# Memory attention of the second block: values as the weights of TensorE, one product per pair of heads

## The chip, the core and the metric

The program runs on one core of one Trainium2 chip. The metric is the device time of one execution in microseconds (us); the median of three runs of the kernel before is 1542.08 us (1541.72 to 1542.87).

## What is computed

Two transformer blocks, one after the other, on 512 tokens of width 1024, all in float32. The change lies in the second block, in the attention of the tokens to a memory of 256 vectors (4 heads of width 64):

```
qm = rmsnorm_2(qm, q_gain).astype(f32)
km = rmsnorm_2(km, k_gain).astype(f32)
logits = jnp.einsum('bqhd,bmhd->bhqm', qm, km) * (MEM_DH_2 ** -0.5)
p = jax.nn.softmax(logits, axis=-1)
out = jnp.einsum('bhqm,bmhd->bqhd', p, vm.astype(f32))
```

Its output (256 columns of the 1024 of `mixed`) is joined with two other mixers' outputs and multiplied by `w_out`: `x = x + mixed @ w_out`.

## The kernel before

Each engine runs its own instruction stream; semaphores order them. TensorE (PE) does nearly all of its work as products of a float32 matrix split in a high and a low part: one tile product is three instructions (L1952 to L1954, in the helper `product`) of 256 or 512 moving columns in the replicated float32 format. Products of plain float32 operands (scores, transposes, values) are issued as two instructions each, transposes as one.

The stretch of the change is the loop `attention("mem_2", ...)` of block 2, written once per engine. It runs in steps s = 0 to 35. There are 32 **units** of (head, tile of 128 queries). Units 0 to 15 are the memory attention ("mem_2"; pairs of heads f = 0, 1, so units 0 to 7 are pair 0), units 16 to 31 the causal attention ("sa"; 1 to 4 tiles of keys each). At step s, in this order:

- PE makes the scores of unit s (L2114; for "mem_2" both heads of a pair at the even steps, L2121 for "sa"), transposes the probabilities of unit s - 3 (L2129) into bank 6, the only transpose bank, makes the value product of unit s - 4 (L2141) in bank 7, the output bank, and then four tile products (12 instructions) of the projections `hi` and `hg` (steps 0 to 31). From step 17 on, `tail` adds pieces of the recurrent mixer at the end of a step, all in bank 1.
- VectorE (DVE) takes the maximum of the scores (L1392, L1394; L1404, L1408 for "sa"), at odd steps divides the outputs of two units by their sums (L1416, L1418) and writes them into `mix`, and then does one round of the top-key search of the sparse mask (L1722, L1723; steps 1 to 22). At steps 4 and 6 it also multiplies `qf` (L1818).
- ScalarE (ACT) copies the transposed probabilities of unit s - 3 from bank 6 to `pT` (L733), takes the exponentials of unit s with their sum (L749), and then does the step's work for the projections: copies, the rounding of a load of weights (L644 at steps 8, 16, 24) and its negation for a DMA that adds (L651).

A value product in the kernel before takes the transposed probabilities of one unit (128 keys x 128 queries, twice) as weights and 64 columns of values as moving operand:

```
for c in range(keys // P):
    v_ = vv(unit, h, c)
    ins = nc.tensor.matmul(B(("O", u_))[:, values(u_, v_.shape[-1])], tb[u_ % 2][:, c, :], v_,
                           start=c == 0, stop=c == keys // P - 1)
```

so its output has tokens on the partitions, and `mix` has to be turned to features for `w_out`. `mix_turn(j)` (L2537, four transposes each) does that for the eight column tiles j: the two of the memory attention, j = 0 and 1, at the ends of steps 32 and 33, the other six after the loop, once DVE has written the last tiles of the recurrent mixer (L1858, semaphore `hg_scaled`).

The attention of block 1 has the other form already: `att_outputs` (L2286, L2293) spreads the inverse sums of a pair of heads over a bank by four transposes, and then uses 64 columns of values as weights and the probabilities as moving operand, the two heads of the pair in the two halves of the output partitions, with c from 0 to 3 and 512, 384, 256 and 128 moving columns.

`plan_banks` numbers the uses of the eight PSUM banks; `claim(key)` waits until the bank's earlier uses are free, `ready(key)` until PE is done with it, `frees(key, ins)` frees it.

## Time and profile before

| | |
|---|---|
| median of 3 runs | 1542.08 us (1541.72 to 1542.87) |
| the profiled execution, its own time | 1541.8 us |
| its span (first to last instruction) | 1540.0 us |
| PE busy | 1521.7 us, 99% |
| DVE busy | 860.6 us, 56% |
| ACT busy | 641.3 us, 42% |
| the loop of the change, PE | about 1030.3 to 1129.7 us |

A row of the timeline gives the start from the beginning of the span, the time until the row's last instruction ends, the engine, the line, the operation and how many instructions were merged. An instruction of PE shows the time until its result is there, and the next one starts long before that; what an instruction costs PE is therefore read from one start to the next, not from its duration. An idle time of over 0.15 us ahead of a row stands in brackets, with what ended it.

### The profile page before, as it was taken

To read this page: it belongs to the slowest core of one execution; us is meant where nothing else is said; L and a number is where in the kernel's file an instruction comes from. 1 tells how busy PE (TensorE), PEld (TensorE's weight loads), DVE (VectorE), ACT (ScalarE), POOL (GpSimd) and SP (SyncE) were. 2 spreads that over 40 slices of the span, in tenths; PEclk is the share of its full clock that TensorE was granted. 3 is DMA by queue.
4 is the path that set the end of the run, shared out by engine and by line. 5 is a ranking of instruction groups with operands and counts; after the bars stand their busy time and mean duration, and the time that the engine had idled before them with its cause. 6 is when DMAs were issued, how large, how long until landed. Compare 5 with 4: busy or idle time off the path is not lost. (4 is left out here: it accounts for less than half of the span.)

```text
span 1540.0 us, 20083 instructions
## 1 busy us (share of the span) xinstructions
PE 1521.7 (99%) x7670; PEld 1268.5 (82%) x7670; DVE 860.6 (56%) x1321; ACT 641.3 (42%) x888; POOL 24.1 (2%) x32
## 2 busy tenths in 40 slices
PE   7999999999999999999999999999999999999999
PEld 7888667888888888888888868999888888888887
DVE  5443565444456877777434778878564543444222
ACT  6442444322245444444333555686653322322210
POOL 0000000000000000000000000010000000000000
PEclk9999999999999999999999999999999999999999
DMA  9313212232233133222333223254312322222232
GB/s 363 132 55 109 103 56 82 83 109 94 98 113 133 55 110 109 83 107 82 137 109 128 69 83 113 56 124 106 91 65 82 110 84 107 87 103 96 95 109 82
DMA packets 25386, 158.33 MB, mean 103 GB/s; under 512 B 2819, under 2 KB 3331, under 8 KB 8300
## 3 DMA queue, kind: packets, MB, share of 16 engines
q1 hardware_dynamic: 23228, 150.01, 27.5%
q0 software_dynamic: 2016, 7.34, 2.5%
q8 instruction: 42, 0.69, 0.2%
q14 instruction: 20, 0.16, 0.0%
q10 hardware_dynamic: 80, 0.13, 0.0%
HBM read 147.87 MB, written 2.13 MB: 97 GB/s over the span
## 5 line engine op out<-in xcount | busy, mean ns | idle before, releaser
L1202 DVE TENSOR_TENSOR w_lo<-raw,w_hi 128x2048 fp32r<-128x2048 f32 x109 | 249.8, 2292 | 347.3 <-ACT w_hi L644 347.2
L1952 PE MATMUL bank<-h_hi,w_hi 128*128 128x512 f32 x1096 | 431.5, 394 | 1.1 <-DVE cy L1544 0.8
L1954 PE MATMUL bank<-h_hi,w_lo 128*128 128x512 f32 x1096 | 427.0, 390 | 0.0
L1953 PE MATMUL bank<-h_lo,w_hi 128*128 128x512 f32 x1096 | 426.7, 389 | 0.0
L644 ACT ACTIVATE w_hi<-raw 128x2048 fp32r<-128x2048 f32 x123 | 235.0, 1910 | 321.7 <-PE bank L1954 307.4
L1952 PEld LDWEIGHTS bank<-h_hi,w_hi 128*128 128x128 f32 x1096 | 205.6, 188 | 45.3 <-issue 2.8
L1954 PEld LDWEIGHTS bank<-h_hi,w_lo 128*128 128x128 f32 x1096 | 205.3, 187 | 43.7
L1953 PEld LDWEIGHTS bank<-h_lo,w_hi 128*128 128x128 f32 x1096 | 205.5, 188 | 42.0 <-issue 0.2
L1952 PE MATMUL bank<-a_hi,w_hi 128*128 128x512 f32 x352 | 136.9, 389 | 0.0
L1953 PE MATMUL bank<-a_lo,w_hi 128*128 128x512 f32 x352 | 136.9, 389 | 0.0
L1954 PE MATMUL bank<-a_hi,w_lo 128*128 128x512 f32 x352 | 136.9, 389 | 0.0
L1952 PE MATMUL bank<-w_hi,h_hi 128*128 128x256 f32 x320 | 97.0, 303 | 0.5 <-ACT tok L682 0.3
L1954 PE MATMUL bank<-w_hi,h_lo 128*128 128x256 f32 x320 | 90.3, 282 | 0.0
L1953 PE MATMUL bank<-w_lo,h_hi 128*128 128x256 f32 x320 | 90.2, 282 | 0.0
L1953 PEld LDWEIGHTS bank<-a_lo,w_hi 128*128 128x128 f32 x352 | 66.1, 188 | 13.8
L1954 PEld LDWEIGHTS bank<-a_hi,w_lo 128*128 128x128 f32 x352 | 66.1, 188 | 13.7
L1952 PEld LDWEIGHTS bank<-a_hi,w_hi 128*128 128x128 f32 x352 | 66.1, 188 | 13.7
L1952 PE MATMUL bank<-br_hi,w_hi 128*128 128x512 f32 (+1 forms) x160 | 62.5, 390 | 0.5 <-DVE br_lo L1272 0.5
L1952 PEld LDWEIGHTS bank<-w_hi,h_hi 128*128 128x128 f32 x320 | 60.9, 190 | 1.9 <-issue 0.7
L1953 PE MATMUL bank<-br_lo,w_hi 128*128 128x512 f32 (+1 forms) x160 | 62.3, 389 | 0.0
L1954 PE MATMUL bank<-br_hi,w_lo 128*128 128x512 f32 (+1 forms) x160 | 62.2, 389 | 0.0
L1953 PEld LDWEIGHTS bank<-w_lo,h_hi 128*128 128x128 f32 x320 | 61.1, 191 | 0.9 <-issue 0.7
(315 smaller groups left out, 2005.2 us busy)
## 6 DMA issues: line engine op xcount, KB each, us to landing
raw<-weights SPq DMA_DIRECT2D x128, 1024.0 KB, 4.8
w_lo<-raw POOLq DMA_DIRECT2D x14, 512.0 KB, 5.0
toep<-bias_scratch SPq DMA_DIRECT2D x8, 448.0 KB, 4.6
x<-xT SPq DMA_DIRECT2D x2, 1024.0 KB, 12.7
x_tok<-x_tok SPq DMA_DIRECT2D x1, 2048.0 KB, 13.8
mem2T<-mem2T SPq DMA_DIRECT2D x2, 1024.0 KB, 5.3
outT<-x SPq DMA_DIRECT2D x8, 256.0 KB, 4.2
lead<-lead SPq DMA_DIRECT2D x2, 512.0 KB, 4.7
```

The costliest lines, as they stand in the source:

```text
L644: nc.scalar.activation(w_hi[PLACE[m]][:, :], raw[m % 2][:, :], ACT.Copy).then_inc(hi_ready, 1)
L1202: nc.vector.tensor_tensor(w_lo[PLACE[m]][:, :], raw[m % 2][:, :], w_hi[PLACE[m]][:, :].bitcast(F32), ALU.subtract).then_inc(lo_ready, 1)
L1952: nc.tensor.matmul(o, lh, rh, start=first, stop=False)
L1953: nc.tensor.matmul(o, lh, rl, start=False, stop=False)
L1954: return nc.tensor.matmul(o, ll, rh, start=False, stop=last)
```

## The change

The 16 value products of the memory attention are taken out of steps 4 to 19. In their place, once per pair of heads f:

- DVE inverts the sums of the pair's eight units and spreads them over 512 columns (`inverse_2`) at steps 9 and 17;
- PE turns that into bank 7 by four transposes ("R2") at the start of steps 10 and 18, and ACT copies the bank into `mix` after the exponentials of the same step;
- PE makes the pair's output ("O2") in the same bank at the start of steps 11 and 19: values as weights (64 columns), probabilities of four query tiles as 512 moving columns, head e in partitions 64e to 64e + 63;
- DVE multiplies the output by the spread inverse sums at steps 12 and 20, in place, in `mix`, which now holds features on the partitions for these two tiles.

The divisions by the sums for these units (L1416, L1418 at the odd steps 5 to 19) are gone, and so are `mix_turn(0)` and `mix_turn(1)`; the rounding of these two tiles reads `mix` instead of a bank. The first value product of "sa" (unit 16, step 20) now waits until bank 7 is freed by DVE's second multiplication.

```diff
@@ -194,8 +194,12 @@
             use(("T", w), T_BANK)
-            if kind == "mem_2":
+            if kind == "mem_2" and s >= SAH * TT:
                 use(("O", w), O_BANK)
+            elif kind == "mem_2":
+                if s % (2 * TT) == 2 * TT - 1:
+                    use(("R2", s // (2 * TT)), O_BANK)
+                    use(("O2", s // (2 * TT)), O_BANK)
             elif s % GROUP[kind] == GROUP[kind] - 1:
@@ -252,7 +256,8 @@
     tiles("o_hg", TT, (TAIL_BANK,))
-    tiles("turn_mix", KT)
+    for j in range(2, KT):
+        use(("turn_mix", j), j % 4)
     tiles("w_out_2", KT, (4, 5, 0, 1), first=FIRST["w_out_2"], per=2)
@@ -395,6 +400,8 @@
         row_2 = [at(f"row_2{s}", AR + (72 + 2 * s) * K, [S]) for s in range(NLP)]
+        pT_pair = [at(f"pT_pair{e}", AR + (20 + 24 * e) * K, [MT, S]) for e in range(2)]
+        inverse_2 = at("inverse_2", AR + 96 * K, [S])
         pT_2 = [at(f"pT_2{s}", AR + (46 + 50 * s) * K, [TT, P]) for s in range(2)]
@@ -432,7 +439,7 @@
         p_ready = sem("p_ready")
-        inverse_ready = sem("inverse_ready")
+        inverse_ready, inverse_2_ready = sem("inverse_ready"), sem("inverse_2_ready")
         bias_saved = sem("bias_saved")
@@ -727,11 +734,19 @@
                         ready(("T", w))
-                        if w >= UNIT0[kind] + 2:
-
-                            ready(("O", w - 2))
+                        unit, h, i, _ = UNITS[w]
+                        if unit == "mem_2":
+                            if w >= UNIT0["mem_2"] + 2 * TT:
+                                ready(("O2", 0))
+                            copy_to = pT_pair[h % 2][:, :, i * P:(i + 1) * P]
+                        else:
+                            if w >= UNIT0["sa"] + 2:
+                                ready(("O", w - 2))
+                            else:
+                                ready(("O2", 1))
+                            copy_to = tb[w % 2][:, 0:keys // P, :]
                         frees(("T", w), nc.scalar.activation(
-                            tb[w % 2][:, 0:keys // P, :], B(("T", w))[:, 0:keys].rearrange("p (c t) -> p c t", t=P),
+                            copy_to, B(("T", w))[:, 0:keys].rearrange("p (c t) -> p c t", t=P),
                             ACT.Copy))
@@ -746,8 +761,18 @@
                         scale = q_root[:, int(unit == "mem_2"), 0, SAH * i + h:SAH * i + h + 1]
+                        total = mx[:, w % 8, 2:3]
+                        if unit == "mem_2":
+                            f = s // (2 * TT)
+                            total = sums[:, f, s % (2 * TT):s % (2 * TT) + 1]
                         nc.scalar.activation(rb[w % NLP][:, 0:keys], src, ACT.Exp, bias=mx[:, w % 8, 1:2], scale=scale,
-                                             accum_out=mx[:, w % 8, 2:3]).then_inc(exp_ready, 1)
+                                             accum_out=total).then_inc(exp_ready, 1)
+                    if s in (2 * TT + 2, 4 * TT + 2):
+                        f = (s - 2) // (2 * TT) - 1
+                        ready(("R2", f))
+                        frees(("R2", f), nc.scalar.activation(
+                            mix[:, :, MIX_MEM + f * P:MIX_MEM + (f + 1) * P],
+                            B(("R2", f))[:, :].rearrange("p (t d) -> p t d", d=P), ACT.Copy))
                     if between is not None:
@@ -1138,7 +1163,12 @@
                 if s > 2 * SAH * TT:
-                    turned("turn_mix", (s - 2 * SAH * TT - 1,), lambda j: mo_hi[:, j, :])
+                    j = s - 2 * SAH * TT - 1
+                    if j < 2:
+                        wait_own(("O2", j))
+                        nc.scalar.activation(mo_hi[:, j, :].rearrange("p (t d) -> p t d", d=P),
+                                             mix[:, :, MIX_MEM + j * P:MIX_MEM + (j + 1) * P], ACT.Copy
+                                             ).then_inc(rounded, 1)
@@ -1407,7 +1437,21 @@
                                                 ).then_inc(neg_max, 1)
-                    if s >= LAG + 1:
+                    if s in (2 * TT + 1, 4 * TT + 1):
+                        f = (s - 1) // (2 * TT) - 1
+                        dve.wait_ge(exp_ready, UNIT0["mem_2"] + 2 * TT * (f + 1))
+                        link(nc.vector.reciprocal(sums[:, f, :], sums[:, f, :]))
+                        nc.vector.tensor_copy(inverse_2[:, :].rearrange("p (u d) -> p u d", d=64),
+                                              sums[:, f, :].unsqueeze(2).to_broadcast([P, 2 * TT, 64])
+                                              ).then_inc(inverse_2_ready, 1)
+                    if s in (2 * TT + LAG + 1, 4 * TT + LAG + 1):
+                        f = s // (2 * TT) - 1
+                        wait_free(("R2", f))
+                        ready(("O2", f))
+                        pair_ = mix[:, :, MIX_MEM + f * P:MIX_MEM + (f + 1) * P]
+                        frees(("O2", f), nc.vector.tensor_tensor(
+                            pair_, B(("O2", f))[:, :].rearrange("p (t d) -> p t d", d=P), pair_, ALU.mult))
+                    if s >= SAH * TT + LAG + 1:
                         w = UNIT0[kind] + s - LAG - 1
@@ -1860,7 +1904,10 @@
                 if s > 2 * SAH * TT + 1:
-                    turned("turn_mix", (s - 2 * SAH * TT - 2,), lambda j: mo_hi[:, j, :], lambda j: mo_lo[:, j, :])
+                    j = s - 2 * SAH * TT - 2
+                    low_part(mo_lo[:, j, :].rearrange("p (t d) -> p t d", d=P),
+                             mix[:, :, MIX_MEM + j * P:MIX_MEM + (j + 1) * P],
+                             mo_hi[:, j, :].rearrange("p (t d) -> p t d", d=P))
@@ -2101,6 +2148,26 @@
                 for s in range(count + LAG + 1):
+                    if s in (2 * TT + 2, 4 * TT + 2):
+                        f = (s - 2) // (2 * TT) - 1
+                        claim(("R2", f))
+                        pe.wait_ge(inverse_2_ready, f + 1)
+                        for i in range(TT):
+                            ins = nc.tensor.transpose(B(("R2", f))[:, i * P:(i + 1) * P],
+                                                      inverse_2[:, i * P:(i + 1) * P], ident[:, :])
+                        done(("R2", f), ins)
+                    if s in (2 * TT + LAG, 4 * TT + LAG):
+                        f = (s - LAG) // (2 * TT) - 1
+                        last = ("T", UNIT0["mem_2"] + 2 * TT * (f + 1) - 1)
+                        claim(("O2", f))
+                        pe.wait_ge(bank_free[slot[last].bank], turn(last) + 1)
+                        for c in range(MT):
+                            for e in range(2):
+                                h = 2 * f + e
+                                ins = nc.tensor.matmul(B(("O2", f))[64 * e:64 * e + 64, :],
+                                                       vm[:, c, h * DH:(h + 1) * DH], pT_pair[e][:, c, :],
+                                                       start=c == 0, stop=c == MT - 1)
+                        done(("O2", f), ins)
                     if LAG <= s < count + LAG and UNITS[UNIT0[kind] + s - LAG][0] == "mem_2":
@@ -2129,7 +2196,7 @@
                         done(("T", u_), ins)
-                    if s >= LAG + 1:
+                    if s >= SAH * TT + LAG + 1:
                         u_ = UNIT0[kind] + s - LAG - 1
@@ -2551,9 +2618,6 @@
                 tail(s - TAIL)
-                if s in (2 * SAH * TT, 2 * SAH * TT + 1):
-                    pe.wait_ge(bank_free[O_BANK], turn(("O", UNIT0["sa"] - 1)) + 1)
-                    mix_turn(s - 2 * SAH * TT)
             wait_all("turn_mq", range(2))
             pe.wait_ge(padded, 4)
```

The line numbers of the changed kernel are higher (L2129 is L2196, L2141 is L2208). Three places in the order of instructions:

**PE, steps 9 to 11.** Before, step 10 begins with the scores (L2114), and each step has transposes (L2129) and a value product (L2141):
```order
L2129 MATMUL bank<-ident,row_m_173 128x128 [waits exp_ready,bank_free6]
L2129 MATMUL bank<-ident,row_m_173 128x128
L2141 MATMUL bank<-vm,pT_180 128x64 [waits bank_free6]
L2141 MATMUL bank<-vm,pT_180 128x64
...
L2114 MATMUL bank<-kmT_even,mqT 128x256 [waits exp_ready,bank_free0]
L2114 MATMUL bank<-kmT_odd,mqT 128x256
L2129 MATMUL bank<-ident,row_m_174 128x128 [waits exp_ready,bank_free6]
L2129 MATMUL bank<-ident,row_m_174 128x128
L2141 MATMUL bank<-vm,pT_179 128x64 [waits bank_free6,bank_free7]
L2141 MATMUL bank<-vm,pT_179 128x64
...
L2129 MATMUL bank<-ident,row_m_171 128x128 [waits exp_ready,bank_free6]
L2129 MATMUL bank<-ident,row_m_171 128x128
```
In the changed kernel (L2196 transposes, L2181 scores):
```order
L2196 MATMUL bank<-ident,row_m_173 128x128 [waits exp_ready,bank_free6]
L2196 MATMUL bank<-ident,row_m_173 128x128
...
L2156 MATMUL bank<-ident,inverse_181 128x128 [waits inverse_2_ready,bank_free7]
L2156 MATMUL bank<-ident,inverse_181 128x128 x3
L2181 MATMUL bank<-kmT_even,mqT 128x256 [waits exp_ready,bank_free0]
L2181 MATMUL bank<-kmT_odd,mqT 128x256
L2196 MATMUL bank<-ident,row_m_174 128x128 [waits exp_ready,bank_free6]
L2196 MATMUL bank<-ident,row_m_174 128x128
...
L2167 MATMUL bank<-pT_pair_179,vm 64x512 [waits bank_free6,bank_free7]
L2167 MATMUL bank<-pT_pair_180,vm 64x512
L2167 MATMUL bank<-pT_pair_179,vm 64x512
L2167 MATMUL bank<-pT_pair_180,vm 64x512
```
The value products are gone; four transposes of `inverse_2` stand ahead of the scores of step 10, and a product of 64 weight columns and 512 moving columns, four times, ahead of the transposes of step 11.

**ACT and DVE, step 10 and what leads to it.** ACT in the changed kernel, from the transposed copy of step 9 to that of step 11:
```order
L748 ACTIVATE pT_pair_179<-bank 128x2x128 [waits bank_ready6]
L768 ACTIVATE row_m_172,sums<-bank,mx,q_root 128x256 [waits bank_ready6,neg_max]
L658 ACTIVATE w_lo_57<-w_hi_55 128x1024 [waits hi_ready]
L748 ACTIVATE pT_pair_180<-bank 128x2x128 [waits bank_ready6]
L768 ACTIVATE row_m_173,sums<-bank,mx,q_root 128x256 [waits bank_ready6,neg_max]
L773 ACTIVATE mix<-bank 128x4x128 [waits bank_ready7]
L689 ACTIVATE v_hg<-bank,st 128x256 [waits bank_ready2]
L658 ACTIVATE w_lo_57<-w_hi_55 128x1024
L748 ACTIVATE pT_pair_179<-bank 128x2x128 [waits bank_ready7,bank_ready6]
```
The copy of "R2" (L773) stands behind the exponentials of step 10 (L768). DVE in the changed kernel, steps 8 to 10:
```order
L1422 TENSOR_REDUCE mx<-bank 128x2 [waits bank_ready5,dve_step]
L1424 TENSOR_TENSOR mx<-mx,q_root 128x2 [waits dve_step]
L1766 MAX st<-sel 128x8
L1767 MATCH_REPLACE sel<-st,sel 128x512 [waits dve_step]
L1443 RECIPROCAL sums<-sums 128x8 [waits exp_ready,dve_step]
L1444 COPY inverse_181<-sums 128x512 [waits dve_step]
L1766 MAX st<-sel 128x8
L1767 MATCH_REPLACE sel<-st,sel 128x512 [waits dve_step]
L1422 TENSOR_REDUCE mx<-bank 128x2 [waits bank_ready0,dve_step]
L1424 TENSOR_TENSOR mx<-mx,q_root 128x2 [waits dve_step]
```
The reciprocal and the spread of the sums (L1443, L1444) stand at step 9, behind the search round of step 8, where L1416 and L1418 stood before.

**DVE and PE, step 20.** DVE in the changed kernel:
```order
L1434 ISA row_175,mx<-bank,sel 128x256 [waits bank_ready6,bank_ready4,dve_step]
L1434 ISA mx 128x1
L1438 TENSOR_SCALAR mx<-mx,q_root 128x1 [waits bank_free4]
L1452 TENSOR_TENSOR mix<-bank,mix 128x4x128 [waits bank_ready7,bank_free7]
L1766 MAX st<-sel 128x8
```
PE in the changed kernel (L2577 is a piece of `tail`, the end of step 19):
```order
L2577 MATMUL bank<-ident,kk 128x128 [waits bank_free1]
L2577 MATMUL bank<-ident,kk 128x128 x3
L2188 MATMUL bank<-skT_even,sqT 128x256 [waits bank_free4]
L2196 MATMUL bank<-ident,row_176 128x128 [waits exp_ready,bank_free6]
L2208 MATMUL bank<-sv,pT_182 128x64 [waits bank_free6,bank_free7]
```
DVE's multiplication (L1452) stands behind the mask and maximum of the scores of step 20 (L1434, L1438), and PE's first value product (L2208) waits for bank 7.

## Rows read from the trace of the kernel before

**Rows 1.** The page, parts 1 and 2: busy time, granted clock
```profile
PE 1521.7 (99%) x7670; PEld 1268.5 (82%) x7670; DVE 860.6 (56%) x1321; ACT 641.3 (42%) x888; POOL 24.1 (2%) x32
...
PEclk9999999999999999999999999999999999999999
```

**Rows 2.** Timeline of PE, step 5 (start us, us, engine, line, op, xcount)
```profile
1040.89 0.28 PE L1954 MATMUL bank<-w_hi,h_lo 128*128 128x256 f32 x1
...
1041.23 0.56 PE L2141 MATMUL bank<-vm,pT 128*128 128x64 f32 x4
...
1041.80 0.28 PE L1953 MATMUL bank<-w_lo,h_hi 128*128 128x256 f32 x1
```

**Rows 3.** Timeline of PE, step 3, which has no value product
```profile
1036.28 0.28 PE L1954 MATMUL bank<-w_hi,h_lo 128*128 128x256 f32 x1
...
1036.73 0.28 PE L1953 MATMUL bank<-w_lo,h_hi 128*128 128x256 f32 x1
```

**Rows 4.** Line L2141 alone: count, ns min/median/max, first and last start
```profile
L2141 PE MATMUL bank<-vm,pT x64: 222/275/275, 1039.1 to 1077.2; 128*128 128x64 f32 x64
```

**Rows 5.** Timeline of PE in block 1, the products of one pair of heads
```profile
196.13 0.65 PE L2293 MATMUL bank<-pT_att,v 128*64 128x512 f32 x2
...
195.60 0.60 PE L2286 MATMUL bank<-ident,inverse 128*128 128x128 f32 x4
196.13 2.38 PE L2293 MATMUL bank<-pT_att,v 128*64 128x512 f32 x16
198.44 0.50 PE L1952 MATMUL bank<-h_hi,w_hi 128*128 128x512 f32 x1
```

**Rows 6.** Timeline of DVE, steps 5 to 9
```profile
1042.77 0.17 DVE L1416 RECIPROCAL mx<-mx 128x2 f32<-128x2 f32 x1
...
1043.24 0.55 DVE L1722 MAX8 st<-sel 128x8 f32<-128x384 f32 x1
...
1050.23 0.69 DVE L1392 TENSOR_REDUCE mx<-bank 128x2 f32<-128x512 f32 x1
...
1052.61 0.17 DVE L1416 RECIPROCAL mx<-mx 128x2 f32<-128x2 f32 x1
```

**Rows 7.** Timeline of PE, DVE and ACT, steps 10 and 12
```profile
1053.25 0.60 PE L2114 MATMUL bank<-kmT_even,mqT 128*128 128x256 f32 x2
...
1054.37 0.44 PE L2129 MATMUL bank<-ident,row_m 128*128 128x128 f32 x2
...
1058.62 0.60 PE L2114 MATMUL bank<-kmT_even,mqT 128*128 128x256 f32 x2
...
1059.48 0.38 PE L2129 MATMUL bank<-ident,row_m 128*128 128x128 f32 x2
...
1059.75 0.69 DVE L1392 TENSOR_REDUCE mx<-bank 128x2 f32<-128x512 f32 x1 [0.64 <-PE bank L2114]
...
1060.74 0.57 ACT L749 ACTIVATE row_m<-bank,mx,q_root 128x256 f32<-128x256 f32 x1 [0.46 <-DVE mx L1394]
```

**Rows 8.** Lines L1370, L851 and L1341 alone, block 1
```profile
L1370 DVE COPY inverse<-sums x4: 426/428/429, 167.1 to 239.3; 128x512 f32<-128x512 f32 x4
...
L851 ACT ACTIVATE spread_inv<-bank x4: 576/577/597, 181.5 to 242.1; 128x512 f32<-128x512 f32 x4
...
L1341 DVE TENSOR_TENSOR q<-bank,spread_inv x4: 680/692/692, 182.1 to 248.0; 128x512 f32<-128x512 f32 x4
```

**Rows 9.** Timeline, step 20
```profile
1079.22 0.60 PE L2121 MATMUL bank<-skT_even,sqT 128*128 128x256 f32 x2
...
1079.95 0.42 DVE L1404 CUSTOM_DVE_ANT_0 row<-bank,sel 128x256 f32<-128x256 f32 x1 [0.56 <-DVE sel L1723]
...
1080.55 0.69 DVE L1722 MAX8 st<-sel 128x8 f32<-128x512 f32 x1
```

**Rows 10.** Timeline, end of the loop
```profile
1127.42 2.18 DVE L1858 SCALAR_TENSOR_TENSOR mix<-mix,st,g_tok 128x128 f32<-128x128 f32 x8
...
1129.65 0.31 PEld L2537 LDWEIGHTS bank<-ident,mix 128*128 128x128 f32 x3 [0.23 <-DVE mix L1858]
```

## The prediction

> **What bounds the kernel now.** I read the page first: PE is busy in 99% of the span at full granted clock, DVE and ACT in 56% and 42% [rows 1]. So every instruction that leaves PE's stream shortens the run by its cost there, and every new wait of PE lengthens it, unless the stretch ends on another engine. Then I read the timeline of the loop that changes. PE's starts follow each other without a hole through nearly all of it; DVE, too, has no hole from 1042.77 to past 1052.61 us [rows 6]. At the loop's end PE waits 0.23 us for DVE's last L1858 [rows 10]. Those two facts decide this case: in the middle a second engine is full, and the end belongs to DVE.
>
> **The sum, part by part**, against the profiled execution's 1541.8 us, which lies 0.3 us under the median.
>
> *Value products taken out.* From the last projection instruction ahead of the transposes to the second one behind them PE takes 0.91 us with a value product (1040.89 to 1041.80) [rows 2] and 0.45 us without (1036.28 to 1036.73) [rows 3]. A unit's value product, four instructions of 64 columns, costs 0.46 us. There are 64 such instructions [rows 4], 16 units: -7.3 us.
>
> *Pair products put in.* The changed kernel has not been seen, but block 1 makes the same product, 64 weight columns, the two heads in two halves of the partitions. The first two of its instructions, 512 columns each, are both done 0.65 us after the first began [rows 5]; one after another two instructions of only 256 columns take 0.60 us [rows 7]. So the two halves run side by side. The 16 instructions are eight side-by-side couples of 512, 512, 384, 384, 256, 256, 128 and 128 columns, 2560 in all, from 196.13 to 198.44: 0.90 ns a column. A pair in the new place has four couples of 512: 2048 x 0.90 = 1.85 us, and 0.09 us ahead of the first (the transposes end at 195.60 + 4 x 0.11 = 196.04). Two pairs: +3.8 us. If the halves ran one after another it would be 4096 columns at 0.84 ns (the scores' 256 columns in half of 0.43 us, from the 0.86 us of the four at 1058.62 to 1059.48 [rows 7]), 3.4 us a pair. I take the first, since it is the same form.
>
> *Sums spread.* Four transposes per pair, 0.11 us each: +0.9 us for two pairs. `mix_turn` 0 and 1, eight transposes of the same size, leave PE: -0.9 us, but at steps 32 and 33. The first transposes behind the loop start at 1129.65 because DVE's eight L1858 run from 1127.42 to 1129.60 without a hole [rows 10], and nothing in DVE's chain waits for `mix_turn`. PE just arrives 0.9 us earlier and waits 0.9 us longer: I cost the removal at 0 (between -0.9, if DVE's chain shortened too, and 0).
>
> *First wait, step 10.* PE gets there six value products earlier: 1053.25 - 6 x 0.46 = 1050.5. It now wants `inverse_2`. DVE has lost L1416 with L1418 of steps 5 and 7, 0.47 us each (1042.77 to 1043.24), so its step 9 begins at 1052.61 - 0.93 = 1051.68; the search rounds and the two `qf` products ahead of it are not shorter, and the scores of step 8 reach DVE in time (it began them at 1050.23, two us behind PE). Reciprocal 0.25 and the spread copy 0.43 us [rows 8]: 1052.4. PE stands still from 1050.5 to 1052.4: +1.9 us. The wait that PE had in this step, 1053.25 + 0.86 to 1054.37, is gone with it: -0.26 us.
>
> *Second wait, step 11.* The pair product needs bank 7, which ACT frees behind the exponentials of step 10. From PE's first scores to DVE's maximum 1.13 us, from there to the exponentials 0.99 us [rows 7], 0.57 us for them, 0.58 us for the copy [rows 8]: 3.3 us after the scores started. PE needs 0.86 us for scores, 0.22 for transposes and 1.43 for twelve projection instructions: 2.5 us. +0.8 us. Of the ACT work queued behind (copy of `v_hg`, negation) nothing is late for PE by more than that.
>
> *The same two at steps 18 and 19.* DVE has lost two more odd-step divisions by then and has no `qf` product: PE's step 12 starts 1.1 us later than before (eight value products of 0.46 less; 0.44 + 1.9 - 0.26 + 0.8 + 1.9 more), at 1059.7. DVE's maximum follows at 1060.9 [rows 7], and up to `inverse_2` of step 17 DVE has, in a row: two maxima of two units (0.87 each), the multiplication of the first pair (0.69 [rows 8]), five search rounds (1.51 each, 1052.61 - 0.87 - 1050.23 [rows 6]), two masked maxima (0.60 at most [rows 9]) and the spread of the sums (0.68): 1072.5 to 1072.8. PE, which loses six more value products on the way, is there at about 1072.2: a wait of 0.3 to 0.6 us, of which I take 0.3 because these masked maxima have half the columns. ACT's copy behind the exponentials of step 18 is 0.8 us late again, as at step 11: together +1.1 us.
>
> *Fifth wait, step 20.* PE's first value product of "sa" needs bank 7 free. Before, DVE reached L1404 0.73 us after the scores' start and the next instruction at 1.33 us [rows 9]. The multiplication stands there now, 0.69 us [rows 8], so the bank is free 2.05 us after the scores' start; PE is ready after 0.54 us: +1.5 us. After that DVE and PE meet again at the end of the same step (DVE waits for the state product), so nothing of it is carried on, up or down.
>
> The sum: -7.3 + 3.8 + 0.9 + 0 + 1.9 - 0.3 + 0.8 + 1.1 + 1.5 = +2.4 us; the tenths are uncertain, and of the places I did not cost (a copy of `kT` behind a later ACT, PE's entry into the half-width product from projections) all can only add, so I say +2.6 us, **1544.7 us** from the median of 1542.1.
>
> A page speaks against the change more strongly. By the Trainium skill, "TensorE: Matmul & The Clock Gate", section "Back-to-back issue gap", a stream of matmuls is spaced by the moving columns, about 60 cycles for up to 64 columns and 518 for 512. By that table alone the 64 instructions would give back an estimated 1.6 us and the sum would come to about +8 us. The same section adds that the load of weights shares in the spacing, and this case's trace shows that side: an instruction of 64 columns is 0.11 us, as much as a transpose of 128.
>
> **The rivals.**
> 1. *The waits don't come.* DVE or ACT are earlier than I think, or the semaphores cost less: then -7.3 + 3.8 + 0.9 - 0.3 = -2.9 us, with the tail's 0.9 us -3.8 us: 1538.3 to 1539.2. For it: DVE is only 56% busy, and three of the waits are guarded by a step's distance. Against: DVE is full in just this stretch, and the copy and the multiplication stand behind work that starts from the same step's scores. Faster by over 0.2%: 0.12, and with some of the waits only, about no change: part of "same".
> 2. *The halves run one after another* in this place: 2 x (3.4 - 1.9) = +3.0 us on top, 1547.7. Against it rows 5. Chance 0.05.
> 3. *The columns decide.* If the old instructions were worth only their columns, 64 x 64 x 0.84 ns = 3.4 us instead of 7.3, the sum would be +6.3: 1548.4. Rows 2 and 3 measure just this difference, so 0.02. This is the case in which the page's table above would hold.
> 4. *The waits come larger*: one in the middle of a saturated DVE pushes the exponentials, and PE waits for its next transposes as well; a lower granted clock after a hole of 1.9 us would do the same (before, the clock stays full throughout [rows 1]). One more wait of 0.8 us puts it beyond the bound: 1545.5 to 1547. Chance 0.28.
> 5. *The change does less than it says*: the turns are gone from the stream but not from the time. That is in my forecast already.
>
> **How the numbers follow.** A measurement of this kernel can tell about 0.2%, 3.1 us, from no change: from 1539.0 to 1545.2. The forecast (all five waits as computed, give or take 0.5 us) has a chance of 0.53, and it lies within the bound, 0.5 us from its upper end. Faster 0.12 from rival 1; slower 0.35 from rivals 2, 3 and 4. The range leaves out the far half of rival 1 and most of rivals 2 and 3: 1540.6 to 1547.6.
>
> **What would show it.** L2141 of "mem_2" gone, steps 4 to 9 of PE 0.46 us shorter each; PE idle before L2156 at step 10, ended by DVE's copy, about 1.9 us; idle before L2167 twice, ended by ACT's copy L773, about 0.8 us; idle before L2208 at step 20, ended by DVE L1452, about 1.5 us; L2167 eight instructions per pair in 1.9 us, couples at the same start; the first transposes behind the loop started by DVE as before, with PE waiting over 1 us. Wrong it is if PE starts L2156 at step 10 without a hole (rival 1), or if eight L2167 take over 3 us (rival 2).

## The result and the profile after

The changed kernel takes **1544.89 us** (median of 14 runs, 1543.72 to 1546.72), the kernel before in the same series 1541.74 us (1541.1 to 1542.87): ratio 1.0021, 95% interval 1.0014 to 1.0028. It is 3.1 us slower, and the interval, 2.2 to 4.3 us, leaves no change out, though the difference is only 0.2% of the time. Predicted were 1544.7 us.

The page of the changed kernel, parts 1 and 2, against [rows 1]:

```profile
span 1543.1 us, 19956 instructions
...
PE 1519.4 (98%) x7622; PEld 1262.5 (82%) x7622; DVE 859.5 (56%) x1311; ACT 641.9 (42%) x890; POOL 24.1 (2%) x32
...
PEclk9999999999999999999999999999999999999999
```

PE has 2.3 us less to do and the span is 3.1 us longer: PE stands still more. The clock is full in every slice, as before. Where it stands still the view of PE's waits says, for 1049 to 1084 us (line <- what it waited for: us in total, times, longest). For the kernel before it lists nothing in the same time.

```profile
PE bank L2156 <- DVE inverse L1444: 1.8, 1, 1.8
PE bank L2208 <- DVE mix L1452: 1.4, 1, 1.4
PE bank L2167 <- ACT mix L773: 1.2, 2, 0.7
```

In the changed kernel the spread transposes are L2156, the pair products L2167, the value products of "sa" L2208, the turns L2604, the three lines of a tile product L1999 to L2001, DVE's spread copy L1444, its multiplication L1452, ACT's copy of the spread sums L773.

The bracket of a row counts from the modelled end of the instruction before. I take a **hole** as start to start less the usual distance: 0.12 us behind a product instruction (see 1050.47 and 1050.59 below), 0.11 behind a transpose. The timeline at the first two places, and what ended each wait:

```profile
1050.47 0.28 PE L1999 MATMUL bank<-w_hi,h_hi 128*128 128x256 f32 x1
1050.59 0.28 PE L2000 MATMUL bank<-w_lo,h_hi 128*128 128x256 f32 x1
1050.71 0.28 PE L2001 MATMUL bank<-w_hi,h_lo 128*128 128x256 f32 x1
...
1051.24 0.68 DVE L1767 MATCH_REPLACE8 sel<-st,sel 128x512 f32<-128x512 f32 x1
...
1051.95 0.20 DVE L1443 RECIPROCAL sums<-sums 128x8 f32<-128x8 f32 x1
1052.19 0.43 DVE L1444 COPY inverse<-sums 128x512 f32<-128x512 f32 x1
...
1052.77 0.30 PE L2156 MATMUL bank<-ident,inverse 128*128 128x128 f32 x1 [1.77 <-DVE inverse L1444]
...
1055.36 0.56 ACT L768 ACTIVATE row_m<-bank,mx,q_root 128x256 f32<-128x256 f32 x1
1055.62 0.28 PE L2001 MATMUL bank<-w_hi,h_lo 128*128 128x256 f32 x1
...
1055.91 0.58 ACT L773 ACTIVATE mix<-bank 128x512 f32<-128x512 f32 x1
...
1056.55 1.94 PE L2167 MATMUL bank<-pT_pair,vm 128*64 128x512 f32 x8 [0.66 <-ACT mix L773]
...
1058.42 0.33 PE L2196 MATMUL bank<-ident,row_m 128*128 128x128 f32 x1
```

Step 10: PE is ready at 1050.71 + 0.12, DVE comes out of its search round at 1051.9, and the transposes start at 1052.77: a hole of 1.94 us. Step 11: 1056.55 - 1055.62 - 0.12 = 0.81 us. The pair product itself takes 1058.42 - 1056.55 = 1.87 us. The same at steps 18 and 19, and step 20:

```profile
1072.22 0.60 PE L2577 MATMUL bank<-ident,kk 128*128 128x128 f32 x4
...
1072.94 0.52 PE L2156 MATMUL bank<-ident,inverse 128*128 128x128 f32 x3
...
1075.27 0.65 PE L2577 MATMUL bank<-ident,kk 128*128 128x128 f32 x4
...
1076.49 1.94 PE L2167 MATMUL bank<-pT_pair,vm 128*64 128x512 f32 x8 [0.57 <-ACT mix L773]
...
1081.10 0.27 PE L2196 MATMUL bank<-ident,row 128*128 128x128 f32 x1
...
1082.00 0.68 DVE L1452 TENSOR_TENSOR mix<-bank,mix 128x512 f32<-128x512 f32 x1
...
1082.73 0.32 PE L2208 MATMUL bank<-sv,pT 128*128 128x64 f32 x1 [1.36 <-DVE mix L1452]
```

Four transposes of L2577 take 0.44 us, so the holes are 1072.94 - 1072.66 = 0.28 us and 1076.49 - 1075.71 = 0.78 us; step 20 has 1082.73 - 1081.21 = 1.52 us. And the end of the loop, which answers to [rows 10]:

```profile
1128.65 0.42 DVE L1894 SCALAR_TENSOR_TENSOR g_tok<-th,g_tok 128x256 f32<-128x256 f32 x1 [0.93 <-ACT th L1151]
1128.99 1.13 DVE L1902 SCALAR_TENSOR_TENSOR mix<-mix,st,g_tok 128x128 f32<-128x128 f32 x4
...
1130.29 0.29 DVE L1462 TENSOR_TENSOR mix<-bank,mx 128x128 f32<-128x128 f32 x1
...
1130.50 2.18 DVE L1902 SCALAR_TENSOR_TENSOR mix<-mix,st,g_tok 128x128 f32<-128x128 f32 x8
1130.64 2.00 PE L2208 MATMUL bank<-sv,pT 128*128 128x64 f32 x16 [0.69 <-DVE mix L1462]
```

The first turn behind the loop starts at 1132.73, right behind DVE's last L1902, as before. PE has a new hole here, ahead of its last value products.

To compare kernels I use the **stretch**: from PE's first scores to the first turn behind the loop. It leaves out what lies ahead of the loop, where all kernels have the same instructions and yet the first scores start anywhere from 1029.4 to 1031.1 us in the profiled executions. The first scores, before and after, and the first turns after:

```profile
1030.29 0.45 PE L2114 MATMUL bank<-kmT_even,mqT 128*128 128x256 f32 x1 [0.47 <-ACT mqT L1026]
...
1030.55 0.45 PE L2181 MATMUL bank<-kmT_even,mqT 128*128 128x256 f32 x1 [0.47 <-ACT mqT L1051]
...
1132.73 0.44 PE L2604 MATMUL bank<-ident,mix 128*128 128x128 f32 x2
```

The stretch is 1129.65 - 1030.29 = 99.36 us before and 1132.73 - 1030.55 = 102.18 us after: **+2.8 us** in the loop, where the sum said +2.4 and the forecast +2.6. The other 0.26 us by which the span is longer lie ahead of the first scores and are no work of the change.

### The profile page after: what moved, and what is told of

Same layout as the page of the kernel before. It is cut to its first block and busy times, and to the rows that moved or that the text cites. A ratio compares the mean times of both kernels' runs of the same rounds, so it can differ in the third digit from the quotient of the medians.

```text
span 1543.1 us, 19956 instructions
## 1 busy us (share of the span) xinstructions
PE 1519.4 (98%) x7622; PEld 1262.5 (82%) x7622; DVE 859.5 (56%) x1311; ACT 641.9 (42%) x890; POOL 24.1 (2%) x32
## 5 line engine op out<-in xcount | busy, mean ns | idle before, releaser
L1999 PE MATMUL bank<-h_hi,w_hi 128*128 128x512 f32 x1096 | 431.4, 394 | 1.1 <-DVE cy L1588 0.8
L2001 PE MATMUL bank<-h_hi,w_lo 128*128 128x512 f32 x1096 | 427.0, 390 | 0.0
L1999 PEld LDWEIGHTS bank<-h_hi,w_hi 128*128 128x128 f32 x1096 | 205.6, 188 | 45.4 <-issue 2.8
L2001 PEld LDWEIGHTS bank<-h_hi,w_lo 128*128 128x128 f32 x1096 | 205.3, 187 | 43.7
L1999 PE MATMUL bank<-a_hi,w_hi 128*128 128x512 f32 x352 | 136.9, 389 | 0.0
L2001 PE MATMUL bank<-a_hi,w_lo 128*128 128x512 f32 x352 | 136.9, 389 | 0.0
L1999 PE MATMUL bank<-w_hi,h_hi 128*128 128x256 f32 x320 | 97.0, 303 | 0.8 <-DMA w_lo<-raw 0.5
L2001 PE MATMUL bank<-w_hi,h_lo 128*128 128x256 f32 x320 | 90.3, 282 | 0.0
L1999 PEld LDWEIGHTS bank<-a_hi,w_hi 128*128 128x128 f32 x352 | 66.1, 188 | 13.8
L2001 PEld LDWEIGHTS bank<-a_hi,w_lo 128*128 128x128 f32 x352 | 66.1, 188 | 13.7
L1999 PE MATMUL bank<-br_hi,w_hi 128*128 128x512 f32 (+1 forms) x160 | 62.5, 390 | 0.5 <-DVE br_lo L1302 0.5
L1999 PEld LDWEIGHTS bank<-w_hi,h_hi 128*128 128x128 f32 x320 | 61.0, 190 | 2.1 <-issue 0.7
L2001 PE MATMUL bank<-br_hi,w_lo 128*128 128x512 f32 (+1 forms) x160 | 62.3, 389 | 0.0
```

The source lines that it names most:

```text
L1999: nc.tensor.matmul(o, lh, rh, start=first, stop=False)
L2001: return nc.tensor.matmul(o, ll, rh, start=False, stop=last)
```

## The experiments

My theory was the sum of the prediction: five waits, and an end of the loop that belongs to DVE. The rivals were that a wait is another one than I said, that it comes back elsewhere when it is taken away, and, for the pair product, that its cost depends on something else than the two halves. Each run was timed in five rounds beside the kernel before. The intervals of the ratios are plus or minus 0.0009, 1.4 us (0.0014 for e11), wider than most effects here; so each verdict goes by the stretch in the trace, and the median stands beside it. A stretch is read from one profiled execution. How well it repeats can be seen in e4 and e7, which left it within 0.02 us of the changed kernel's.

| kernel | stretch, us | against after | median, us | before in that series | ratio |
|---|---|---|---|---|---|
| before | 99.36 | -2.82 | | | 1 |
| after | 102.18 | 0 | 1544.89 | 1541.74 | 1.0021 |
| e1 | 101.31 | -0.87 | 1544.16 | 1542.15 | 1.0015 |
| e2 | 102.15 | -0.03 | 1544.79 | 1542.15 | 1.0018 |
| e3 | 100.60 | -1.58 | 1543.46 | 1542.15 | 1.0010 |
| e4 | 102.20 | +0.02 | 1544.78 | 1542.15 | 1.0020 |
| e5 | 101.48 | -0.70 | 1544.05 | 1542.13 | 1.0012 |
| e6 (on before) | 99.03 | | 1541.80 | 1542.13 | 0.9998 |
| e7 | 102.19 | +0.01 | 1545.07 | 1542.13 | 1.0019 |
| e11 | 105.60 | +3.42 | 1549.06 | 1542.13 | 1.0041 |
| e8 | 99.68 | -2.50 | 1543.17 | 1542.21 | 1.0007 |
| e9 | 97.50 | -4.68 | 1540.26 | 1542.21 | 0.9987 |
| e10 (on before) | 98.74 | | 1541.50 | 1542.21 | 0.9996 |
| e12 | 96.93 | -5.25 | 1539.41 | 1541.99 | 0.9983 |

### e1: ACT's copy of the spread sums first

```diff
 for s in range(count + LAG):
+    if s in (2 * TT + 2, 4 * TT + 2):
+        f = (s - 2) // (2 * TT) - 1
+        ready(("R2", f))
+        frees(("R2", f), nc.scalar.activation(
+            mix[:, :, MIX_MEM + f * P:MIX_MEM + (f + 1) * P],
+            B(("R2", f))[:, :].rearrange("p (t d) -> p t d", d=P), ACT.Copy))
```

The same lines leave their place behind the exponentials.

> Edit: in steps 10 and 18 ACT copies the spread sums (R2) out of bank 7 before anything else of the step, not behind the exponentials. Theory (the second and fourth wait are ACT's copy standing behind the exponentials of the same step): the holes of 0.81 and 0.74 us ahead of L2167 shrink to what the copy of the last transposes leaves; from the durations in the trace I get about 1.0 us less in all (some 0.5 us each), so about 1.0 us below the changed kernel, ratio to before 1.0015. Rival (PE there waits for the transposed probabilities of step 10, the copy L748, and not for R2's): both holes stay, 0.0 us.

Stretch 0.87 us shorter. PE's waits, 1049 to 1084 us:

```profile
PE bank L2156 <- DVE inverse L1444: 1.8, 1, 1.8
PE bank L2208 <- DVE mix L1452: 1.4, 1, 1.4
PE bank L2167 <- ACT pT_pair L754: 0.2, 1, 0.2
```

The two waits for L773 are gone from the list, and what is left is for the copy of the last transposed probabilities (here L754). By the starts more is left than the list shows: 1056.00 - 1055.58 - 0.12 = 0.30 us ahead of L2167 in step 11 and 0.40 us in step 19, where the changed kernel has 0.81 and 0.78. Of each, 0.09 us is no wait: e9 and e12 show that much ahead of every pair product. So the second and fourth wait were what I said for about 0.9 of their 1.4 us; behind the copy that was moved stands ACT's next one, and the other 0.5 us is for that.

### e2: DVE's spread copy a step earlier

```diff
-if s in (2 * TT + 1, 4 * TT + 1):
-    f = (s - 1) // (2 * TT) - 1
+if s in (2 * TT, 4 * TT):
+    f = s // (2 * TT) - 1
```

> Edit: DVE forms inverse_2 one step earlier, in steps 8 and 16, right behind the maxima and ahead of the search round. Theory A, that this wait can simply be taken away: the hole of 1.93 us ahead of L2156 at step 10 and the 0.28 us at step 18 go, and the kernel is about 2.0 us faster than the changed one (1542.9). Theory B, that ACT is the next limit (between steps 7 and 10 it also has the rounding of the next weights, 1.9 us, and two negations): the hole ahead of L2156 goes, but holes of the same sum appear ahead of the transposes of step 10 and of L2167, and the time stays at the changed kernel's within 0.3 us. I expect B.

No change. PE's waits:

```profile
PE bank L2167 <- ACT mix L773: 1.5, 2, 0.9
PE bank L2208 <- DVE mix L1452: 1.4, 1, 1.4
PE bank L2196 <- ACT pT_pair L748: 1.0, 1, 1.0
PE bank L2156 <- DVE inverse L1444: 0.3, 1, 0.3
```

The largest wait fell from 1.8 to 0.3 us, and the run is as long as before: a new wait of 1.0 us stands ahead of step 10's transposes, and the one ahead of the pair product grew. ACT's timeline in this kernel shows why:

```profile
1051.27 1.91 ACT L651 ACTIVATE w_hi<-raw 128x2048 fp32r<-128x2048 f32 x1
1053.07 0.38 ACT L748 ACTIVATE pT_pair<-bank 128x256 f32<-128x256 f32 x1
...
1053.50 0.33 PE L2196 MATMUL bank<-ident,row_m 128*128 128x128 f32 x1 [0.97 <-ACT pT_pair L748]
```

The rounding of the next weights (step 8) holds the copy that frees the one transpose bank. By the starts the holes of steps 10 and 11 are 0.43, 1.13 and 1.10 us, 2.66 together, against 1.94 + 0.81 = 2.75 in the changed kernel. In step 18 the hole of 0.28 us goes, and 0.21 us turn up ahead of the next transposes of the tail (L2577), which start when ACT's L1161 ends. Theory B.

### e3: the second multiplication at the end of step 19

```diff
-if s in (2 * TT + LAG + 1, 4 * TT + LAG + 1):
+if s in (2 * TT + LAG + 1, 4 * TT + LAG):
```

> Edit: DVE multiplies the second pair's outputs at the end of step 19, ahead of the search round, not in step 20 behind the scores' masked maximum. Theory (the fifth wait is this multiplication, which frees bank 7 for the first value product of block 2's own attention): the hole of 1.52 us ahead of L2208 at step 20 goes, and nothing takes its place: about 1.5 us below the changed kernel. Rival (PE and DVE meet again within step 20 and 21, so that a wait of DVE turns up behind it): 0.0 to 0.5 us.

Stretch 1.58 us shorter. The multiplication now starts before step 20 and L2208 follows the transposes at once:

```profile
1078.65 0.68 DVE L1452 TENSOR_TENSOR mix<-bank,mix 128x512 f32<-128x512 f32 x1
...
1080.40 0.27 PE L2196 MATMUL bank<-ident,row 128*128 128x128 f32 x1
...
1080.51 0.33 PE L2208 MATMUL bank<-sv,pT 128*128 128x64 f32 x2
```

The rival falls: nothing took the wait's place.

### e4: the loops of the pair product exchanged

```diff
-for c in range(MT):
-    for e in range(2):
+for e in range(2):
+    for c in range(MT):
```

> Edit: the pair product's loops are exchanged, so that the four instructions of one half of the partitions stand ahead of the four of the other, with the same instructions, operands and results. Theory (halves that follow each other run side by side, and that is why a pair costs 1.87 us): a pair takes 3.4 us, eight instructions of 512 columns at 0.43 us each, and the kernel is about 3.1 us slower than the changed one, 1548.0. Rival (the time belongs to the form, 64 weight columns, not to the neighbour in the other half): no change, 1544.9.

**My theory falls.** The pair takes the same time, and the next row starts 1.87 us later as before:

```profile
1055.46 1.94 PE L2167 MATMUL bank<-pT_pair,vm 128*64 128x512 f32 x8 [0.65 <-ACT mix L773]
1057.33 0.44 PE L2196 MATMUL bank<-ident,row_m 128*128 128x128 f32 x2
```

The records still come in couples, 14 ns apart (7 ns in the changed kernel), although the partner stands four instructions further on. Either the halves work beside each other in this order of the stream too, or 64 weight columns cost half of 128. e11 tells these apart.

### e11: both heads into one half

```diff
-ins = nc.tensor.matmul(B(("O2", f))[64 * e:64 * e + 64, :],
+ins = nc.tensor.matmul(B(("O2", f))[0:64, :],
                        vm[:, c, h * DH:(h + 1) * DH], pT_pair[e][:, c, :],
-                       start=c == 0, stop=c == MT - 1)
+                       start=c == e == 0, stop=c == MT - 1 and e == 1)
```

> Edit: the changed kernel's eight instructions of each pair product all write the same 64 partitions of the bank, as one sum, so that the two heads' outputs are added up and the upper half keeps what was in it (the outputs of block 2's memory attention are wrong therefore). Exchanging the loops (e4) left the time as it was, and its records show the two halves' instructions starting in couples 14 ns apart although they stand four instructions apart in the stream. Theory A (each half of the partitions works through its own instructions, beside the other): with all in one half a pair takes 8 x 0.43 = 3.4 us, 3.1 us more than the changed kernel in all, 1548.0. Theory B (an instruction with 64 weight columns takes half the time of one with 128, whatever stands beside it): 1.87 us per pair as now, 0.0 us.

```profile
1057.13 3.65 PE L2167 MATMUL bank<-pT_pair,vm 128*64 128x512 f32 x8 [0.65 <-ACT mix L773]
1060.71 0.44 PE L2196 MATMUL bank<-ident,row_m 128*128 128x128 f32 x2
```

3.58 us instead of 1.87 for the same eight shapes; the stretch is 3.42 us longer, twice the difference. Theory A: the price hangs on the two halves of the output partitions, not on the shape and, by e4, not on which of these two orders the product has. The edit changes one thing more: the eight products are added up in one place, not four in each of two. That this costs something isn't seen, since 0.43 us from one start to the next for 512 columns is the pace of the scores in [rows 7] (256 columns in 0.215 us); two separate sums within one half were not tried.

### e5 and e6: DVE's order at the loop's end, in both kernels

```diff
+if NORM_HG + 2 <= s < NORM_HG + 2 + TT:
...
 if s % 2 == 0 and 18 <= s <= 32:
...
```

The block with the four scalings of one tile, in front of the gate's product instead of behind it.

> Edit to the changed kernel, nothing of the change itself: in step 32 DVE scales the second tile of the hg heads (four L1902) ahead of the gate's product L1894 instead of behind it. Theory (the stretch's end is DVE's, which is why the two turns that left PE's stream gave nothing): DVE stands idle from about 1127.75 to 1128.65 us for ACT's last Tanh in that step, so the four scalings fit in there; the first transposes behind the loop start about 0.7 us earlier than in the changed kernel, until PE's own work (its last value products) is the limit, and the kernel is 0.7 us faster (1544.2). Rival (PE's last value products and the turns set the end by themselves): 0.0 us.

> The same exchange in the kernel before, where PE still makes two turns in steps 32 and 33. Theory: PE waits only 0.23 to 0.26 us for DVE at the loop's end there, so the exchange can give about 0.25 us and no more (1541.9); against e5 this tells how much of the 0.9 us of the two turns the changed kernel can take once DVE is out of the way: about 0.5 us. Rival (the turns cost nothing whatever DVE does): the same gain in both.

The changed kernel gains 0.70 us, the kernel before 0.33. So of the 0.9 us that the two turns cost PE, 0.37 us can be had once DVE is faster here (expected were about 0.5); the rest still lies behind DVE, which ends the stretch in e5 too:

```profile
1129.16 0.42 DVE L1904 SCALAR_TENSOR_TENSOR g_tok<-th,g_tok 128x256 f32<-128x256 f32 x1
...
1130.24 2.18 DVE L1896 SCALAR_TENSOR_TENSOR mix<-mix,st,g_tok 128x128 f32<-128x128 f32 x8
...
1132.48 0.33 PE L2604 MATMUL bank<-ident,mix 128*128 128x128 f32 x1
```

### e7: the two turns put back

The edit also gives the two turns their uses of the banks again; those lines are left out here.

```diff
+if s in (2 * SAH * TT, 2 * SAH * TT + 1):
+    j = s - 2 * SAH * TT
+    pe.wait_ge(bank_free[O_BANK], turn(("O2", j)) + 1)
+    mix_turn(j)
+    pe.sem_inc(bank_free[slot["turn_mix", j].bank], 1)
```

> Edit: the changed kernel with the eight transposes of the first two mix tiles put back on PE in steps 32 and 33 (as before the change); nobody reads their outputs. Theory (they lie in front of a wait for DVE): the hole of 0.86 us ahead of L2208 and the one of 0.26 us ahead of the first turn behind the loop shrink by 0.9 us together, and the time is the changed kernel's within 0.2 us. Rival (every instruction in PE's stream costs its time): 0.9 us slower, 1545.8.

Stretch 102.19 us against 102.18: eight transposes for nothing, as the forecast had it. What shrank is the new hole alone; the transposes fill it, and PE's wait for L1902 stays, 0.26 us.

### e8: the three moves together

> Edit: the moves of e1, e2 and e3 together in the changed kernel (ACT's copy of the spread sums first in its step, DVE's inverse_2 in steps 8 and 16, the second multiplication at the end of step 19). The stretch from the first scores to the first transposes behind the loop took 102.18 us in the changed kernel, 101.31 in e1, 102.15 in e2, 100.60 in e3, and 99.37 in the kernel before. Theory (the waits of steps 10 and 11 belong to ACT's round work of steps 7 to 10, and e2's move adds nothing beside e1's): e1's 0.87 and e3's 1.58 add up and the rest stays, 99.7 us, some 0.4 us above the kernel before. Rival (the moves help each other, for instance since DVE's inverse_2 and ACT's copy are two halves of one wait): 98.5 us or less, below the kernel before.

99.68 us, where adding e1 and e3 to the changed kernel gives 102.18 - 0.87 - 1.58 = 99.73: e2's move is worth nothing beside them as well. PE's waits that are left are ACT's, but for one:

```profile
PE bank L2196 <- ACT pT_pair L754: 1.0, 1, 1.0
PE bank L2167 <- ACT pT_pair L754: 0.7, 2, 0.5
PE bank L2156 <- DVE inverse L1444: 0.3, 1, 0.3
```

### e9, e10 and e12: the rounding two steps later

```diff
-if s in (8, 16, 24):
+if s in (10, 18, 26):
     round_w(FIRST["hi"] + s // 8 + 1)
 for part in range(2):
-    if s - part in (1, 9, 17, 25):
+    if s - part in (1, 11, 19, 27):
```

e9 is e8 with this and with e5's exchange; e10 is the kernel before with this and the exchange.

> Edit: e8, and ACT rounds the next weights (L651) two steps later, in steps 10, 18 and 26, with its negations behind (steps 11 and 12, and so on), and DVE's exchange of e5 at the loop's end. Theory (the rounding, 1.92 us on ACT in step 8, is what the waits of steps 10 and 11 come from once inverse_2 is early; with it behind ACT's copy of step 10 nothing of either wait is left but 0.4 us): the stretch takes 97.0 us less 0.7 us of the exchange, 96.3 to 96.5 us, 3 us under the kernel before: 1539.0, ratio 0.998. Rival (the later rounding makes the negations, the addition by DMA or the next load late, and PE waits for weights): a hole ahead of the first product instructions of step 16 or 24, and 1541 or more.

> The control of e9: the kernel before with those of e9's edits that it can have (the rounding two steps later and the exchange at the loop's end). Theory: its own loop has 0.25 us to gain from either, so 0.5 us at most, 98.9 us for the stretch and 1541.6; what e9 gains beyond this belongs to the changed product. Rival (the rounding held the kernel before back too): 1.5 us or more, as near to e9 as that makes it.

e9's stretch is 97.50 us, where I expected 96.3 to 96.5: most of the gain came, and with it the rival's hole. Of the 2.18 us between e8 and e9, 0.70 are e5's by its own run; the rest is the rounding's, and the waits ahead of L2196 and L2167 that e8 had are gone from the list. The hole:

```profile
1067.35 0.39 PE L1999 MATMUL bank<-w_hi,h_hi 128*128 128x256 f32 x1 [0.64 <-DMA w_lo<-raw]
```

e10 gained 0.62 us, a little over the 0.5 that its theory allowed and far from the rival's 1.5. e9 lies 1.24 us below it in the stretch. To remove the hole, e12 puts the rounding into an idle time of ACT in step 10, ahead of the exponentials:

```diff
+if s == 10:
+    round_w(FIRST["hi"] + 2)
 if s < count:
```

> Edit: e9, with the first of the late roundings put ahead of step 10's exponentials on ACT instead of behind them and the copy of v_hg. In e9 it began at 1055.82 us, though ACT stood idle from 1053.25 to 1054.91 for DVE's maximum; the negations and the two additions by DMA came behind it (issued at 1060.04 and 1062.15), and the first product instruction of step 16 waited 0.80 us for the second of them. Theory: the rounding moves into that idle time, the additions come some 2 us earlier, the hole of 0.80 us at step 16 goes and nothing takes its place: stretch 96.7 us instead of 97.50, time 1539.5. Rival (the exponentials of step 10, now 0.3 us later or more, delay PE's transposes and scores): a new hole in steps 10 to 13 that takes half of it or more, 1540.0 or above.

Stretch 96.93 us, where 96.7 was expected, median 1539.41 us, ratio 0.9983, interval 0.9974 to 0.9992. The wait for the addition is not in the list of PE's waits any more:

```profile
PE bank L2158 <- DVE inverse L1446: 0.3, 1, 0.3
```

But it has only become too short for the list:

```profile
1067.05 0.38 PE L2198 MATMUL bank<-ident,row_m 128*128 128x128 f32 x2
1067.48 0.39 PE L2001 MATMUL bank<-w_hi,h_hi 128*128 128x256 f32 x1
```

From the two transposes to the product instruction behind them it is 0.43 us here, 1.02 us in e9 (1066.33 to 1067.35) and 0.14 us where nothing is waited for (1049.18 to 1049.32 in the changed kernel). So 0.29 of the 0.88 us are left, and the difference, 0.59 us, is the gain of e12 over e9.

The working behind it was half right. The first addition came 1.1 us earlier, the second didn't: it was issued at 1062.88 in a stretch that began at 1031.14, 31.74 us in, and at 1062.15 with a beginning of 1030.42 in e9, 31.73 us in. What shortened the hole is that this second addition landed sooner, 4.6 us behind its issue instead of 5.2, with the two issued 3.2 us apart and not 2.1. That they hindered each other in e9 was not tried apart, and their distance alone doesn't settle it: in the kernel before, the addition issued at 1077.50, 2.7 us behind the one before it, took 6.5 us.

## Why the prediction was right, point by point

| term of the sum | said | measured |
|---|---|---|
| 16 value products out | -7.3 | -7.15 (0.447 each) |
| two pair products | +3.8 | +3.7 (1.87 each) |
| spread transposes | +0.9 | +0.9 |
| turns out of steps 32 and 33 | 0 | 0 (e7) |
| wait at step 10, and the old one gone | +1.9 - 0.3 | +1.94 - 0.25 |
| wait at step 11 | +0.8 | +0.81 |
| waits at steps 18 and 19 | +1.1 | +0.28 + 0.78 |
| wait at step 20 | +1.5 | +1.52 |
| sum | +2.4 | +2.55 by these rows, +2.8 by the stretch |

The 0.447 us is the step from one unit's transposes to the next, after less before, both counted from the first scores: unit 1's start at the same time in both kernels, unit 6's 2.23 us earlier after the change, in five equal steps, against 0.46 in [rows 2, 3]. The difference of the two kernels stands at +2.81 us from unit 18's transposes on, and stays there for ten units: nothing behind step 20 adds or gives back, as the prediction had it for the fifth wait. The 0.27 us between the two sums lie mostly in steps 19 and 20, which are 0.1 us longer each than their holes and instructions say; why is not shown. The forecast had added 0.2 us for places that it did not cost, so it met this number, but by a guess.

The Trainium skill, "TensorE: Matmul & The Clock Gate", section "Back-to-back issue gap", has the table of about 60 cycles for up to 64 moving columns for a single matmul, and says of a stream of weight loads and matmuls that both set the distance. The prediction's estimated +8 us took the table alone. The measured 0.447 us for four instructions, 0.11 us each, as much as a transpose of 128 columns, are not the table's distance and agree with what the section says of a stream.

*What was right for its reason.* The waits were found at their places, ended by the engines named. For the wait of step 20 the cause is whole: take it away (e3) and the time goes. For those of steps 11 and 19 ACT is the engine, as said, but the place of its one copy is worth only 0.9 of their 1.4 us (e1); the rest went when ACT's rounding was moved as well (e9). The end of the loop belongs to DVE, shown by e5 to e7.

*What was right with a weaker reason.* The wait at step 10 is DVE's, as said, but it is not worth its 1.9 us: without it (e2) ACT's rounding takes the same time. The prediction counted it as DVE's alone; two engines were late together, and the sum needed only one of them. It would have been wrong as a guide to a repair.

*What was wrong.* None of it is in a term that the sum needed. First, the reading behind the rival "the halves run one after another": I took [rows 5] for neighbours in the stream that overlap; e4 shows that they need not be neighbours. That rival's price was too low as well: "3.4 us a pair" was 3.58 in e11. Second, I said that the first transposes behind the loop would wait over 1 us. They have a hole of 0.26 us as before; the other 0.9 us appeared ahead of the last value products instead (0.69 in the bracket), where L2208 waits for DVE's L1462, which stands behind the same scalings. The value, 0, was right. Third, taken at 0 between 0 and -0.9, the turns are worth 0.37 us as soon as DVE's order is better.

The rival "the waits come larger" (0.28) did not come: no further wait that costs time, no lower clock (full in all 40 slices), and the waits as large as computed. That the median, 1544.89 us, lies 0.2 us from the forecast is closer than the method: the sum was short by 0.4 us in the loop, and two medians of the kernel before, 1541.74 and 1542.21, differ by more than that.

## What to carry to other kernels

Before a wait is counted as the cost, ask what else is due in the same 2 us: e2 removed the largest wait on the list, 1.8 us, and gained nothing, while e3 removed a smaller one and gained all of it. What to look for is whether another engine holds something that PE needs just behind. A product that gathers many small outputs in one large one moves the release of its bank to a few points; where these stand in the other engines' streams decided more here than the product did. It saves PE 2.5 us of instructions (7.15 - 3.74 - 0.88), and the waits took 5.1 us. With the same instructions in better places (e12) it is 2.6 us faster than the kernel before, 2.4 by the stretch. Those two of e9's moves that the kernel before can have give it 0.7 us (e10), which can't be told from nothing; the earlier place of the rounding in e12 was not tried there.

## What was not expected of the hardware

Two products with 64 weight columns into the two halves of the output partitions run side by side not only alternating but also when four instructions of one half stand ahead of the four of the other: 1.87 us for eight instructions of 512 columns either way (e4), against 3.58 us when all write one half (e11), 0.43 us from start to start. A float32 product with 128 x 64 weights and 512 moving columns costs 0.45 us when its half works alone and 0.23 us when the other half has work four instructions further on. How far apart the two may stand was not tried.
